# Opening of the first layer: five plain products on TensorE ahead of the first projection, and five VectorE steps of the state-space rotation moved behind the scaling of the tiles

## What is computed

```python
h = rmsnorm(x, p['g_mix'][l]) * (1.0 + sc_m) + sh_m      # shift and scale from cs @ w_ada
proj = h @ p['w_in'][l]                                  # u, qkv, z, ...
# s5_ssm
dt = jnp.exp(log_dt)[:, None]
mag = jnp.exp(lr * dt)
ab_re = mag * jnp.cos(li * dt)
ab_im = mag * jnp.sin(li * dt)
# ... k_re, k_im from ab_re, ab_im, lr, li
p_re, p_im, s_re, s_im = lax.associative_scan(_cplx_combine, (a_re, a_im, bu_re, bu_im), axis=1)
```

## Time and profile before

| | us |
|---|---|
| median of 3 runs | 1893.74 |
| lowest and highest | 1890.24, 1894.74 |
| the profiled execution, time | 1896.73 |
| its span, first to last instruction | 1894.6 |
| PE busy in the span | 1847.5 (98%) |
| DVE, ACT, POOL busy | 734.4, 445.8, 241.9 |
| mean granted clock of PE | 0.984 |

### The profile page before, as it was taken

One profiled execution on the slowest core, in us unless ns is written; L12 is line 12 of the kernel. 1 busy time (PEld: TensorE's weight loads), 2 busy tenths in 40 slices (PEclk: granted clock), 3 DMA queues, 4 the chain that ended last, 5 costly groups with the idle time before them and its releaser, 6 DMA issues.

```text
span 1894.6 us, 55454 instructions
## 1 busy us (share of the span) xinstructions
PE 1847.5 (98%) x24876; PEld 1377.1 (73%) x24876; DVE 734.4 (39%) x1579; ACT 445.8 (24%) x843; POOL 241.9 (13%) x281
## 2 busy tenths in 40 slices
PE   7999999999999999999899999999999999999997
PEld 3778898899999778898866666666666666666665
DVE  5896548655575696548500100101101011100112
ACT  2214334545433224334310000000010000000101
POOL 2641423000001541423100000000000000000000
PEclk8999998999999999998999999999999999999999
DMA  9486444555553356444489999999989999999993
GB/s 359 174 281 249 155 152 158 199 183 184 178 170 130 123 201 219 144 157 163 159 339 383 395 381 394 381 386 391 387 317 379 385 393 384 389 378 395 375 398 125
DMA packets 143141, 525.47 MB, mean 277 GB/s; under 512 B 16192, under 2 KB 16704, under 8 KB 142272
## 3 DMA queue, kind: packets, MB, share of 16 engines
q1 hardware_dynamic: 140544, 508.82, 72.1%
q10 hardware_dynamic: 1728, 7.85, 1.2%
q0 software_dynamic: 640, 5.35, 0.7%
HBM read 515.52 MB, written 6.43 MB: 275 GB/s over the span
## 4 chain that ended last, share of the span: by engine, by line
PE 93%; DVE 4%; issue 1%; ACT 1%; DMA 1%; SPq 0%; DVEq 0%; ACTq 0%
PE bank L1066 46%; PE bank L911 13%; PE bank L297 11%; PE bank L651 8%; PE bank L515 4%; PE bank L531 2%; PE bank L1074 1%; PE bank L480 1%; PE bank L996 1%; PE bank L432 1%; DMA ring<-in_w 1%; DVE ulo L2077 1%; PE bank L457 1%; PE bank L895 0%; PE bank L1004 0%
## 5 line engine op out<-in xcount | busy, mean ns | idle before, releaser
L1066 PE MATMUL bank<-ring,arena 128*32 128x256 f32 x16128 | 877.3, 379 | 0.0
L1066 PEld LDWEIGHTS bank<-ring,arena 128*32 128x32 f32 x16128 | 520.7, 110 | 344.7 <-issue 2.3
L297 PE MATMUL bank<-hT,ring 128*128 128x264 f32 x864 | 205.7, 398 | 5.2 <-ACT hT L1245 5.2
L2443 DVE TENSOR_TENSOR arena<-arena,bank 128x128 f32<-128x128 f32 x168 | 38.2, 283 | 424.5 <-ACT arena L1572 424.5
L297 PEld LDWEIGHTS bank<-hT,ring 128*128 128x128 f32 x864 | 166.8, 196 | 41.3 <-issue 12.1
L1572 ACT ACTIVATE arena<-bank 128x128 f32<-128x128 f32 x168 | 34.4, 277 | 448.7 <-PE bank L1066 448.7
L911 PE MATMUL bank<-hh,whi 128*128 128x264 f32 x448 | 128.0, 286 | 2.1 <-DVE hl L2473 1.5
L911 PE MATMUL bank<-hh,wlo 128*128 128x264 f32 x448 | 126.9, 283 | 0.0
L911 PE MATMUL bank<-hl,whi 128*128 128x264 f32 x448 | 126.9, 283 | 0.0
L2465 DVE TENSOR_TENSOR wlo<-ring,whi 128x1024 fp32r<-128x1024 f32 x84 | 102.2, 1224 | 61.4 <-ACT whi L1458 61.3
L2351 DVE COPY arena<-bank 32x256 f32<-32x256 f32 x24 | 10.2, 427 | 291.6 <-PE bank L1066 291.3
(11 more groups left out here) (423 smaller groups left out, 2487.1 us busy)
## 6 DMA issues: line engine op xcount, KB each, us to landing
ring<-in_w SPq DMA_DIRECT2D x964, 512.0 KB, 5.9
out_gdns<-arena POOLq DMA_DIRECT2D x2, 2048.0 KB, 8.6
arena<-in_gdn ACTq DMA_DIRECT2D x2, 1536.0 KB, 7.3
xT<-in_x ACTq DMA_DIRECT2D x1, 1056.0 KB, 9.0
out_y<-hT SPq DMA_DIRECT2D x4, 264.0 KB, 2.0
arena<-in_gdn ACTq DMA_DIRECT2D x2, 512.0 KB, 4.3
masks<-in_masks ACTq DMA_DIRECT2D x1, 512.0 KB, 11.1
cpk<-in_cpk SPq DMA_DIRECT2D x1, 512.0 KB, 5.4
```

The lines of the kernel that those rows point to most:

```text
L297: ins = pe.matmul(out, w, rhs, start=start, stop=stop)
L1066: ins = pe.matmul(o[32 * j:32 * j + 32, 0:DQ], x(t), w[:, DQ * c:DQ * c + DQ], start=first, stop=last)
L2443: ins = v.tensor_tensor(erow[:, c % 3, r, :], srow[:, c % 2, r, :], up_bank(c, r)[:, P:2 * P], ALU.mult)
```

## The change

PE opens one more bank after the transposes of layer 0 and runs five products of `ones` with tiles of `xT` into it, 128x264 each; nobody reads the result. On DVE the last five steps of `s5_rotation` become a function of their own, `s5_rotation_end`. In layer 0 it is called behind `norm`, ahead of `s5_factor`; in layer 1 right after `s5_rotation`, as before.

```diff
@@ -556,6 +556,11 @@
                     ada_slots(ADA_S // 2)
                     pe.wait_ge(ld["masks"], 16)
                     ada_turn(0, 0)
+                    name = ("warm", "mix", 0)
+                    ps = open_bank(pe, name, 0)
+                    for i in range(5):
+                        ins = pe.matmul(ps[:, 0:N], ones[:, :], xT[:, i, :], start=True, stop=True)
+                    close(ins, name)
                 else:
                     rms(("mix", l))
 
@@ -1700,6 +1705,9 @@
                     tt(o, o, x2, ALU.mult)
                     ts(o, o, a, None, ALU.add)
                 tt(o, o, x, ALU.mult)
+
+            def s5_rotation_end(l):
+
                 tt(si, c_(11), c_(12), ALU.mult)
                 ts(si, si, 2.0, None, ALU.mult)
                 tt(co, c_(12), c_(12), ALU.mult)
@@ -2192,6 +2200,7 @@
                     ada_mod(0, 0)
                 norm(l, "mix", "g_mix", 0)
                 if l == 0:
+                    s5_rotation_end(0)
                     s5_factor(0)
                     s5_gain(0)
                     s5_gain_imag(0)
@@ -2524,6 +2533,7 @@
                     s5_angle(1)
                 if s == UP_S + 15:
                     s5_rotation(1)
+                    s5_rotation_end(1)
                 if s == UP_S + 18:
                     s5_factor(1)
                 if s == UP_S + 21:
```

## The result

| | before | after |
|---|---|---|
| median of 6 runs each, us | 1894.24 (1890.24 to 1897.07) | 1903.47 (1900.45 to 1904.83) |
| ratio, 95% interval | 1 | 1.0046 (1.0035 to 1.0056) |
| the profiled execution | 1896.73, span 1894.6 | 1904.83, span 1902.8 |
| PE busy | 1847.5 | 1851.0 |
| mean granted clock of PE | 0.984 | 0.986 |

The change makes the kernel 0.46% slower, 9.2 us by the medians. A second set of six runs of the same kernel gave 1902.13 against 1894.6, ratio 1.0046 (1.0032 to 1.0060), 7.5 us. The forecast was 1899.8 with an upper end of 1902.5. The sign and the mechanism held; the size did not.

The account below looks back on a forecast made before the run. PE, busy 98% of the span, was taken as the bound. Hidden gains of 0.63 and 2.0, 4.65 of the tables' 4.9 reaching PE and 1.5 by the clock gave +6.1: 1893.74 to 1899.8 us, range 1895.0 to 1902.5.

Parts of the forecast that it names:

- the seven banks: PE's banks go round in seven; each group waits for the one seven before, slack 2.2 us at the second `bu`.
- tables' delay: POOL's tables in layer 0: starting 4.78 us later, they end 4.9 us later, with ends of -0.7 and 5.5.
- the slow stretch: POOL's 14 table steps beside DVE's 128x512 products in before: 10.08 us, 0.72 each against 0.33 earlier.
- the fifteen steps: POOL's table steps still behind at 51.94: expected to cost between 0.33 us each (4.8) and 0.56 (8.3).
- The bank's share at the third `bu`: PE's third `bu` waits for pair 3's bank, freed late by DVE: not before 109.95 against 105.30, 4.65 us.
- the same fall there: PE's clock halves behind the wait at the second `bu`, as near 60 before: 5.7 to 6.6 us late, mean 6.1.
- this gain of 2.6 nor a loss of 1.9: Opening: PE gains 0.63 plus 2.0 us, or half-clock products delay it 1.9; both hidden in the second `bu`'s wait.
- the 6.1 stay to the end: Behind the third `bu`: PE is later than DVE's delay, no other DVE wait grows, +6.1 us remains.
- The stall without a fall of the clock: Rival at the second and third `bu`: the bank wait alone, +4.65 us, 1898.4; chance 0.22.
- POOL keeping its pace: Rival in the tables: they end 0.7 us earlier, PE keeps at most 0.95 us, 1892.8; chance 0.13.
- end at half clock: Rival in the opening: first projection up to 1.9 us later, swallowed by the wait; forecast's time, no separate chance given.
- The rival with a longer low clock: Rival behind the second `bu`: low clock lasts through two stretches between `bu`s, another 2 us, 1902; chance 0.08.

Follow-up runs that it names:

- early tables: After, with layer 0's rotation ahead of the norm's root on DVE and exponential `mag` behind it: 1890.56 us, ratio 0.998 to before; without the five products 1893.84, 0.9991.
- thirteen products: After, with 13 more plain 128x264 products filling PE's wait ahead of the second `bu`: 1901.1 us against before's 1894.6, ratio 1.0034.
- move alone: After without the five plain products, only the five rotation steps moved: 1900.24 us against before's 1894.64, ratio 1.0028.
- short tables: After, with POOL's six products of the 16-entry turn in layer 0 replaced by two memsets: 1896.05 us against before's 1895.26, ratio 1.0008.
- tables late: Before, with POOL's layer 0 tables also waiting for the eighth scaled tile, DVE's order untouched: 1899.45 us against 1894.64, ratio 1.0030.
- products alone: Before with the five plain products added, rotation steps not moved: 1894.83 us against 1894.64, ratio 0.9998.
- nine products in the wait: After, with nine more plain 128x264 products in PE's wait ahead of the second `bu`: 1900.28 us against before's 1895.26, ratio 1.0023.
- move alone, again: After without the five plain products, unedited, run again on one chip with after: 1901.36 us, ratio 1.0035 to before.
- tables late and products: Before with the five plain products, and POOL's layer 0 tables held until the eighth scaled tile: 1899.83 us against 1894.6, ratio 1.0030.
- after, again: The kernel after, unchanged, run and profiled a second time: 1902.13 us against before's 1894.6, ratio 1.0046.

## Why the prediction was right, and where it was wrong

**Right, to a tenth or two.** The modulation was to start at 31.65 and did at 31.66; POOL's first copy at 37.2, measured 37.17; the first projection at 34.1 with a clock of 1.00, measured 34.05, and 14.48 us for the 64 instructions against 14.8 worked out. PE was to reach the second `bu` at 80.4; its idle stretch before 85.16 began at 80.49 (85.16 - 4.67). That the moved steps are harmless on DVE and costly on POOL, that the seven banks pass the delay to PE in front of the second `bu`, and that the clock falls there: all of it stands in the rows of after, and the kernels with late, short and early tables confirm the cause.

**The tables' delay, over-sized.** 4.9 us were expected, 4.26 measured: POOL started 4.73 us late and made up 0.47 on its way. In the slow stretch it took 0.67 us a step (15 in 9.98), where the trace of before has 0.72. DVE's products, which the prediction left in their place, began at 41.19 instead of 41.86. (Its bounds for the fifteen steps are a little off too: 15 x 0.33 is 4.9 to 5.0 and not 4.8, 15 x 0.56 is 8.4 and not 8.3.) The bank's share at the third `bu`, 4.65 in the sum, is 3.9 (thirteen products).

**The clock, under-sized.** The step "the same fall there" gave 1.5 us beyond the bank's share. Measured are 2.5 (111.74 - 109.20). The 32 instructions behind the wait lost 2.54 us (9.93 - 7.39), not 1.1 to 2.0. The length of the low stretch, 10.2 us where the prediction had 6.6, is not the whole reason: in the move alone it was 6.8 us, but it began at 87.95, behind the `bu` products and in a second wait, so that it fell on the projections. They took 10.28 us, and the third `bu` came at 111.86, as late as in after. What a low stretch costs depends on what lies in it. The two errors, in the bank and in the clock, nearly cancel, and that is luck: +6.1 was expected at the third `bu`, +6.44 and +6.87 came.

**"Neither this gain of 2.6 nor a loss of 1.9 is seen at the end: both only change how long that wait is."** This sentence took the length of the wait to be free of charge. One execution of each kernel:

| kernel | PE's waits at the second `bu` and behind it | low clock after it | third `bu` |
|---|---|---|---|
| thirteen products in the wait | none, 1.1 | none | 109.20 |
| short tables | 0.8 + 1.1 | 3.4 | 106.18 |
| tables late | 1.0 + 1.1 | 3.4 | 110.54 |
| products alone | 1.3 + 1.1 | 6.8 | 108.12 |
| move alone | 1.8 + 1.1 | 6.8 | 111.86 |
| nine products in the wait | 2.4 | 6.8 | 110.70 |
| move alone, again | 3.1 | 6.8 | 110.55 |
| tables late and products | 3.2 + 0.2 | 6.8 | 110.15 |
| after | 4.7 | 10.2 | 111.74 |
| after, again | 5.0 | 10.2 | 112.17 |

The longest waits of PE stand beside the longest low clock. But the low clock is the same behind waits of 1.3 and of 3.2 us, and the third `bu` does not follow it; nor do the times, in which the products added 0.8 us to the move and 0.4 to the late tables. That the gain of 2.6 us cost time by lengthening the wait is therefore possible and not shown. The Trainium skill (TensorE: Matmul & The Clock Gate, "What's actually happening") was cited for a price that varies from run to run, since the gate's observation isn't aligned with the kernel's start. Two executions of the move alone agree with that: the clock fell 2.6 us behind the start of the second `bu` in one and 0.3 us in the other, and the third `bu` came at 111.86 and 110.55. Two of after differ less (111.74, 112.17).

**"Afterwards PE is later than DVE's delay, so no other wait on DVE can grow, and the 6.1 stay to the end."** This is the step that failed. Against +6.4 to +6.9 at the third `bu` stand +9.2 and +7.5 us in the medians; the 12 runs of after average 1902.9, some 8 us over the medians of before. And another wait on DVE did grow: at the third `bu` of layer 1, PE of the first execution of after waits for a bank that was free in time in before.

```profile
685.66 0.50 PE L480 MATMUL bank<-uT,arena 32*128 32x128 f32 x4 [1.36 <-DVE arena L1861]
```

Layer 1 opened at the full clock there (14.48 us for its first 64 projection instructions, 16.16 before), PE came to the bank earlier within the layer, waited, and the clock fell again (3.4 us from 688.40): the pattern of layer 0 on a smaller scale. From the start of layer 1 to the experts it lost 1.0 us net; another 0.67 us came between the third `bu` and the end of the projection loop, where the chain passes through a transfer into the ring (8.04 us from 147.36). The second execution waits 0.15 us at that bank and lost 2.5 us of its delay on the way. All engines from the third `bu` to the end, before and then the first execution of after:

```profile
105.30:1894.60 1789.30, 1758.84 (x24095) 1319.51 (x24086) 656.37 (x1385) 419.26 (x789) 197.56 (x190) 0.99 0.75 278
111.74:1902.80 1791.06, 1757.21 (x24095) 1317.75 (x24086) 655.95 (x1384) 419.31 (x789) 194.93 (x189) 0.99 0.75 277
```

PE is busy 1.6 us less and idle 3.4 us more, and the mean clock of the whole execution is higher than before's (0.986 against 0.984). So in this execution the loss behind the third `bu` is waiting, and not later falls of the clock.

Over all launches the clock has its part. On the chip of the second set, before's 17 launches have a mean granted clock of 0.9872 and a mean time of 1894.8, after's six 0.9855 and 1902.6, the ten with thirteen products 0.9879 and 1900.8. By an estimate from these means a launch of after spends 6.7 us more at half clock than one of before (2 x (1 - clock) x time), which costs at most half of that, 3.3 of the 7.8 us between the means; the sum had 1.5. The kernel with thirteen products has no more low clock than before and is still 6.0 us slower, though its third `bu` is only 3.9 late. Where the 1 to 3 us between the third `bu` and the medians arise is open; no run here isolates it. Another 0.5 us of the miss is the starting point: the median of before was 1893.74 in three runs and 1894.24 in six, 1894.6 to 1896.31 in the later sets.

**The rivals.** The stall without a fall of the clock (1898.4) did not occur in after; the kernel with thirteen products is that case made by hand, and it took 1901.1. POOL keeping its pace is refuted by the 0.67 us a step. The products did not end at half clock. The rival with a longer low clock (1902), at a chance of 0.08, was nearest in time. It was priced as a second fall; what came was one low stretch 3.4 us longer. The range ended at 1902.5, 8.8 us above the starting median; the forecast's own spread, which ended at 7.5, rested on a single length of low clock and on a delay that changes no more behind the third `bu`.

## What to carry to other kernels

Before steps are moved out of one engine's critical stretch, follow each semaphore that they post and ask what the waiting engine's list feeds; steps for which nobody waits (the exponential here) are the ones to move. Time won on an engine that then waits for another was worth nothing here. A wait can bring a fall of the clock behind it; price that from every low stretch in the trace and from what will lie in it, not from the nearest one. A delay that has been followed to one point is not yet the delay at the end: behind it, the same ring of banks made PE wait again. Speed up the list that ends last first: the same products that brought nothing before took part in a gain once the tables started early.

## What the runs showed of the hardware

**A busy PE did not bring the clock back at once.** Behind the wait of after the clock was at half for 10.2 us; of the 10.1 us shown above PE was busy in 9.18, at first with products on 32 rows and then with full ones. In the kernel with nine products it was 6.8 us behind a wait of 2.38, and the fall itself came only at 85.78, 0.5 us after PE had resumed.

**POOL's narrow steps of 16, 32 and 64 elements take the same time beside DVE's wide products.** Steps of POOL in after, the first ahead of DVE's 128x512 products of two tiles, the others beside them:

```profile
40.92 0.23 POOL L2596 TENSOR_TENSOR arena<-arena,pw 128x16 f32<-128x16 f32 x1
...
42.76 0.65 POOL L2578 TENSOR_TENSOR pw<-pw 128x16 f32<-128x16 f32 x1
...
47.61 0.65 POOL L2596 TENSOR_TENSOR arena<-arena,pw 128x32 f32<-128x32 f32 x1
```

A step of 128x64 took 0.65 us there too, in before at 44.24, and 0.30 without such a neighbour (51.86 in after). 0.65 us is nearly the 0.69 us of one such DVE product, whose own time does not change there. In the kernel with early tables, wider steps of POOL meet the same products, and then DVE pays too:

```profile
44.13 0.69 DVE L1637 TENSOR_TENSOR ckk<-cpk,sm 128x512 f32<-128x512 f32 x1
44.85 0.99 DVE L1637 TENSOR_TENSOR sx<-cpk,sm 128x512 f32<-128x512 f32 x1
```

```profile
44.29 1.01 POOL L2600 TENSOR_TENSOR arena<-arena,pw 128x256 f32<-128x256 f32 x1
```

The Trainium skill (SBUF — State Buffer, "Who interferes with whom") says that a DVE instruction with two inputs in SBUF contends with a GpSimd instruction that reads SBUF. Both rows agree with it. The narrow steps lost time alone; the wide ones, 0.62 us where DVE's products were narrow (60.40 in after), lost time and took some from DVE.
